# Conv matrices in pieces of 1 KB, five buffers for them in the second half of the convolution, and Silu pairs one group earlier

## The reference, cut to what matters

```python
def reference(x, ...):
    u = rms_norm(h, mix_pre_g)
    proj = u @ w_in                                    # 1024 -> 5120 columns
    a, gate = split(proj[..., :2048])
    c = a * sigmoid(gate)                              # GLU, 1024 channels
    c = depthwise_causal_conv(c, dw_kernel, dw_bias)   # 31 taps
    c = silu(layer_norm(c, conv_ln_g, conv_ln_b))
    y_conv = c @ w_conv_out
    y_pool = (pooled means of proj[..., 2048:3072]) @ pool_w * pool_scale @ w_pool_out
    g_conv, g_pool = sigmoid(proj[..., 3072:4096]), sigmoid(proj[..., 4096:])
    merged = g_conv * y_conv + g_pool * y_pool
    h = h + rms_norm(merged @ w_o, mix_post_g)
    v = square(relu(rms_norm(h, mlp_pre_g) @ w_ff1)) @ w_ff2
    return h + rms_norm(v, mlp_post_g)
```

## Time and profile before

| | us |
|---|---|
| median of 3 runs (lowest, highest) | 972.39 (970.23, 973.51) |
| the profiled execution's own time | 973.2 |
| its span, first to last instruction of the slowest core (core 7) | 971.6 |
| spans of cores 0 to 7 | 967.3, 962.5, 964.5, 968.4, 967.3, 964.5, 963.5, 971.6 |
| TensorE busy in that span | 947.4 (98%) |
| queue q0 (POOL): packets, MB | 55136, 46.45 |
| queue q1 (SP): packets, MB | 69792, 64.05 |

### The profile page before, as it was taken

The page is one execution under the profiler, slowest core; times in us unless marked ns, Lnnn a source line. Parts: engine busy times, 40 slices in busy tenths (PEclk is TensorE's granted clock), DMA queues, the critical chain, the costliest instruction groups (busy, mean ns, idle before and its releaser), DMA issues.

```text
span 971.6 us, 14273 instructions; the slowest of 8 cores (962.5 to 971.6 us)
## 1 busy us (share of the span) xinstructions
PE 947.4 (98%) x4990; PEld 479.7 (49%) x4990; DVE 405.3 (42%) x651; ACT 326.8 (34%) x592; POOL 42.4 (4%) x50
## 2 busy tenths in 40 slices
PE   5999999999989999999999999999999999999997
PEld 3555666775544444444444444444444444444444
DVE  3364232332647415675665541344323442333222
ACT  3565322111102492565544341133312341223211
POOL 3001000010110000010101000000000000000000
PEclk9999999999989999999999999999999999999999
DMA  9999602999999759569879994310242014210021
GB/s 193 217 218 177 77 1 46 138 155 144 126 121 177 131 123 148 112 143 234 152 195 177 201 177 109 98 65 1 66 127 93 19 26 116 96 47 1 1 87 66
DMA packets 125144, 111.69 MB, mean 115 GB/s; under 512 B 56945, under 2 KB 107377, under 8 KB 125074
## 3 DMA queue, kind: packets, MB, share of 16 engines
q0 software_dynamic: 55136, 46.45, 35.3%
q1 hardware_dynamic: 69792, 64.05, 25.7%
q10 hardware_dynamic: 146, 0.27, 0.1%
HBM read 127.78 MB, written 16.84 MB: 149 GB/s over the span
## 4 chain that ended last, share of the span: by engine, by line
PE 94%; DMA 4%; ACT 1%; issue 1%; DVE 0%; POOL 0%; DVEq 0%; ACTq 0%; POOLq 0%
PE ps L342 93%; DMA arena<-w_in 2%; DMA arena<-convw 2%; ACT arena L355 1%; PE ps L345 1%; ACT L355 0%; DVE arena L375 0%; POOL arena L378 0%; DVE arena L365 0%; DVEq L173 0%; ACT tmpA L355 0%; ACT junkb L355 0%; ACTq L140 0%; DVEq L140 0%; DVE sm L369 0%
## 5 line engine op out<-in xcount | busy, mean ns | idle before, releaser
L342 PE MATMUL ps<-arena 128*128 128x512 bf16 (+2 forms) x4560 | 916.8, 364 | 9.6 <-DMA arena<-convw 4.2
L342 PEld LDWEIGHTS ps<-arena 128*128 128x128 bf16 x4560 | 454.7, 104 | 464.3 <-issue 15.4
L355 ACT ACTIVATE tmpA<-ps 128x512 f32<-128x512 f32 x226 | 133.7, 595 | 343.2 <-PE ps L342 331.3
L358 DVE TENSOR_TENSOR arena<-tmpA 128x512 bf16<-128x512 f32 x128 | 88.2, 692 | 112.1 <-ACT tmpA L355 112.1
L358 DVE TENSOR_TENSOR arena<-ps,tmpA 128x512 bf16<-128x512 f32 x64 | 44.0, 691 | 151.8 <-ACT tmpA L355 133.5
L355 ACT ACTIVATE junkb<-ps 128x512 bf16<-128x512 f32 (+1 forms) x65 | 38.4, 591 | 177.5 <-DVE tmpA L358 112.7
L358 DVE TENSOR_TENSOR tmpA<-ps,gbt 128x512 f32<-128x512 f32 (+1 forms) x65 | 44.3, 681 | 34.3 <-PE ps L342 28.9
L355 ACT ACTIVATE junkb<-arena 128x1024 bf16<-128x1024 f32 (+1 forms) x33 | 34.6, 1050 | 60.6 <-DMA arena<-out 50.6
L358 DVE TENSOR_TENSOR sm<-sm 128x1 f32<-128x1 f32 x33 | 5.3, 160 | 108.5 <-ACT junkb L355 108.5
L355 ACT ACT_TABLE_LOAD x35 | 44.9, 1283 | 10.9 <-DVE mv L671 3.1
L355 ACT ACTIVATE arena<-ps 128x512 bf16<-128x512 f32 (+1 forms) x58 | 33.2, 586 | 36.2 <-PE ps L342 34.0
(11 more groups left out here) (40 smaller groups left out, 143.2 us busy)
## 6 DMA issues: line engine op xcount, KB each, us to landing
arena<-xh SPq DMA_DIRECT2D x32, 512.0 KB, 8.7
arena<-w_ff POOLq DMA_DIRECT2D x16, 1024.0 KB, 25.0
out<-arena SPq DMA_DIRECT2D x31, 512.0 KB, 3.0
arena<-out SPq DMA_DIRECT2D x28, 512.0 KB, 3.8
arena<-convw POOLq DMA_DIRECT2D x16, 768.0 KB, 13.0
arena<-w_in POOLq DMA_DIRECT2D x4, 1024.0 KB, 67.0
arena<-w_in POOLq DMA_DIRECT2D x2, 2048.0 KB, 22.6
arena<-w_in POOLq DMA_DIRECT2D x4, 512.0 KB, 20.3
```

Source lines behind the costliest of these rows:

```text
L342: kb.op("pe", lambda e: e.matmul(out_ap, lhsT=lhsT, rhs=rhs, start=start, stop=stop, skip_group_check=skip), reads=reads, writes=writes)
L355: kb.op("act", lambda e: e.activation(out=out_ap, in_=in_ap, func=func, **kw), reads=reads, writes=writes)
L358: kb.op(eng, lambda e: e.tensor_tensor(out=out_ap, in0=in0, in1=in1, op=op), reads=reads, writes=writes)
```

## The change

Three edits. The pieces of a conv load become twice as long (2 KB of f32, which land as 1 KB of bf16). Two more buffers for conv matrices are placed in the region of `S[1]`, which is free once the second GLU is done; loads 11 and 12 go there and are issued together ahead of the second half of the convolution, behind load 10 on POOL's queue. From load 8 on, load `w + 5` is issued behind `w`, and loads 13, 14 and 15 go to buffers 2, 0 and 1. Loads 0 to 10 keep their buffers and places. The load of `w_conv_out` waits for load 15 as before, which is now in buffer 1. The Silu pairs move to behind groups 22, 25, 28 and 30.

```diff
-        Wc = [aview(OFF_C + 4608 + b * 3072, 3072, g=8, d=3, n=128) for b in range(3)]
+        WC_OFF = [OFF_C + 4608, OFF_C + 7680, OFF_C + 10752, OFF_S + 8192, OFF_S + 11264]
+        Wc = [aview(o, 3072, g=8, d=3, n=128) for o in WC_OFF]
...
-        for b in range(3):
-            kb.reg(("Wc", b), (OFF_C + 4608 + b * 3072, 3072))
+        for b in range(5):
+            kb.reg(("Wc", b), (WC_OFF[b], 3072))
...
+        def wc_buf(w):
+            return {11: 3, 12: 4, 13: 2, 14: 0, 15: 1}.get(w, w % 3)
+
+        def cload(out_ap, in_ap, keys, after=()):
+            kb.op("pool", lambda e: e.dma_start(out=out_ap, in_=in_ap, max_dma_last_dim=2048), writes=keys, dma=True, after=after)
+
         def wc_load(w):
-            kb.op("pool", lambda e: e.dma_start(out=Wc[w % 3].rearrange("p g d n -> p (g d n)"), in_=convw[w // 2][:, (w % 2) * 3072:(w % 2 + 1) * 3072],
-                                                max_dma_last_dim=1024), writes=[("Wc", w % 3)], dma=True)
+            cload(Wc[wc_buf(w)].rearrange("p g d n -> p (g d n)"), convw[w // 2][:, (w % 2) * 3072:(w % 2 + 1) * 3072], [("Wc", wc_buf(w))])
...
-            if q % 2 == 1 and w + 3 < 16:
-                wc_load(w + 3)
+            nw = w + (3 if w < 8 else 5)
+            if q % 2 == 1 and nw < 16:
+                wc_load(nw)
...
         side1.pop(0)()
         side1.pop(0)()
+        wc_load(11)
+        wc_load(12)
         interleave(groups[:12], side1, 3)
-        wload(S[1][:, :, :], wco_v, ["wco"], after=[kb.last_write[("Wc", 0)]])
+        wload(S[1][:, :, :], wco_v, ["wco"], after=[kb.last_write[("Wc", 1)]])
...
-            if n in (23, 26, 29, 31):
-                i = (n - 22) // 3
+            if n in (22, 25, 28, 30):
+                i = (n - 21) // 3
                 silu_pair(i)
```

More of the change, by code:

```diff
@@ L652, in cv_mm @@
             w = cc * 2 + q // 2
+            wb = wc_buf(w)
             b = nb()
@@ L656, in cv_mm @@
                 for d in range(3):
-                    MM(ps[:, b, g4 * 128:(g4 + 1) * 128], UTt[bf][:, gl, 14 + d:142 + d], Wc[w % 3][:, gl % 8, d, :], d == 0, d == 2,
-                       [("UT", bf), ("UTh", bf), ("Wc", w % 3)], [PSK(b)])
+                    MM(ps[:, b, g4 * 128:(g4 + 1) * 128], UTt[bf][:, gl, 14 + d:142 + d], Wc[wb][:, gl % 8, d, :], d == 0, d == 2,
+                       [("UT", bf), ("UTh", bf), ("Wc", wb)], [PSK(b)])
             dst = ru[:, cc, :].rearrange("p (r g c) -> p g r c", r=16, g=16)[:, q * 4:q * 4 + 4, :, :]
```

## The result

The changed kernel takes 981.25 us (981.02 to 981.42, 4 runs); the kernel before takes 972.53 us beside it. The ratio is 1.0093, 95% interval [1.0075, 1.0111]: slower by 0.9%, where 969.1 us was forecast. The sets ran on different chips, so two experiments are compared by their ratios and not by their times.

What follows compares the result with a forecast made beforehand. TensorE's waits for loads, transposes and ScalarE on the four slowest cores were taken as the bound. After gains and a 2.2 us transpose price core 4 ends at 967.5, plus 1.6 between span and time: 969.1 us, range 964.5 to 976.0.

Steps and rivals of the forecast that it cites:

- The turn-taking: DMA engines alternate packet by packet between queues with work, so each transpose packet beside a load waits for one piece.
- part 2: Loads 11 and 12 beside the transposes of blocks 4 and 5: block 4's lands 2.2 us later on the slow cores.
- a share of 45%: Part of block 4's transpose taken to run beside a load, from core 0's packets: 0.45 x 4.9 = 2.2 us.
- the first rival: Block 4's transpose is paired with load pieces all along: price 4.9 us on cores 0 and 4, 975.1 us; chance 0.22.
- The slower rival: The packet pairs themselves are slow, 152 ns each, delaying block 4's transpose by 10.5 us: 980.7 us; chance 0.15.
- The step that failed: First half of the convolution: no load is added and half as many pieces are mixed in, so the cost is nothing.
- A second term: Block 5's transpose, used about 9 us after block 4's: loads and transposes are over by then, so no cost.
- the sum: Gains subtracted on cores 7, 3, 0 and 4, with 2.2 us added on cores 0 and 4; core 4 slowest at 967.5.
- The clock: Low clock behind core 7's block 7 stall: 3.4 us of TensorE's full-speed time lost, to be regained.
- Part 1's gain: Five buffers remove the convw stalls: 4.15 and 3.4 us of clock on core 7, 4.0 on core 3, about 1 elsewhere.
- parts 1 and 3: Five buffers end the convw waits; Silu pairs one group earlier end the 0.96 us ScalarE wait on all four cores.
- the fourth rival: Block 7's stall stays, for its transpose: 1.6 us and the lower clock on core 7, 969.7 us; chance 0.05.

Runs made afterwards that it cites:

- Experiment 6: The changed kernel with 1 KB landed pieces for loads 0 to 9 only, 512 bytes from load 10 on: 974.7 us, ratio 1.0023 to the kernel before.
- experiment 1: The changed kernel with pieces back at 512 bytes landed, five buffers and new Silu order kept: 968.86 us, ratio 0.9966 to the kernel before.
- experiment 5: The changed kernel with its pieces doubled once more, to 2 KB landed: 1005.95 us, ratio 1.0341 to the kernel before.
- experiment 2: The kernel before with only the pieces lengthened to 1 KB landed, three buffers and old Silu order kept: 982.7 us, ratio 1.0113.
- Experiment 7: The changed kernel with 512-byte landed pieces for loads 0 to 9, 1 KB from load 10 on: 975.6 us, ratio 1.0036 to the kernel before.
- Experiment 9: The changed kernel with 512-byte landed pieces and load 15 held until block 7's transpose lands: 967.3 us, ratio 0.9948 to the kernel before.

## Why the prediction was wrong

**Right.** The waits for `convw` and for ScalarE went, load 14 was issued at 249.34 us on core 7, and nothing waited for `w_conv_out`, whose load came 5.6 us earlier on core 7 and 4.8 later on core 4 (13 earlier was told). The turn-taking is as told, and its rate with 1 KB pieces, 148 a us, was measured as 147.

**Right by luck.** Block 4's transpose took 2.2 us longer on core 4 (15.4 to 17.6), the very figure of part 2. Over the eight cores it is 2.2 to 6.4, 3.4 on the mean, and core 3, where the price was to be nothing, now waits 3.86 us. The figure rests on a share of 45% read from one stretch of core 0; in the changed kernel the queues run nearly side by side through most of the transpose (1492 and 1649 packets from 238 to 250 us on core 4), as the first rival told. The slower rival had the sign and nearly the time (980.7), but its mechanism was a rate of 105 pairs a us, which isn't what happened.

**The step that failed** is the sentence "In the first half no load is added, and half as many pieces are mixed in: nothing." Its term was 0 and measured 5.5 us. The price of a longer piece was charged only where loads are added. But q1 takes turns with q0 wherever both have work, and block 2's transpose has loads beside it already before the change, with the halo's 16-byte packets ahead of it on its own queue. Experiment 6, which differs from experiment 1 in the pieces of loads 0 to 9 alone, gives the 5.5 us. That longer pieces cause it is shown; that the slower pace of the pairs is all of it is not, since on the slowest cores some 4 us of block 2's delay pass in the near standstill. The half of the sentence that sounds like a gain, fewer pieces to mix in, found no support: in experiment 5, with half as many pieces once more, the wait at block 2 grew to 15 us on three cores.

**A second term** was set to nothing: block 5's transpose "over by then". It stands behind block 4's on q1 and has loads 11 and 12 beside it, which the change itself put there; on core 4 it was 26.3 us on its way against 13.2 before. The placement alone lengthens it from 12.6 to 17.4 us on the mean of the cores, the long pieces then to 22.5 (table in experiment 2). It had more room than was told, too: block 5 comes about 13 us behind block 4 before the change (on core 7 the loads behind their first halves are issued at 244.30 and 257.34 us), not 9, because the reckoning left out the time of the `cv_mm` themselves. Experiment 7 gives 6.8 us for blocks 4 and 5 together, against 2.2 in the sum.

**The clock** was mis-sized in both directions. For the stall taken away on core 7 I took 3.4 us; but 10 us from its end have a clock of 0.72, so that only 2.8 were lost in work, the rest in idle time:

```profile
278.70:288.70 10.00, 10.00 (x70) 5.88 (x71) 3.38 (x6) 0.60 (x1) 1.12 (x2) 0.72 0.48 72
```

For the stalls put in the forecast took none, and each of core 4's three cost 1.7 to 2.7 us.

**Part 1's gain** was too large: 6.3 us for parts 1 and 3 together on the slowest core, 3.3 measured with small pieces. With small pieces the fourth rival, given 0.05, is what happened: load 14 comes in time and block 7's transpose holds TensorE for 2 to 4 us on five cores. Experiment 9 shows it in the traces, by holding load 15 back. (In the changed kernel itself the waits ahead of block 7 hide this one.) The 14.5 us on record for that transpose were seen, and explained away.

**The sum was made for four named cores of one run.** Core 7 was the slowest of that run and seldom of another (7 of 60), so the distance "to the next core" is no bound on what a change can gain or lose; what counts is how often any of the eight meets a late transfer.

What stays open: why some transposes crawl beside a load queue that moves next to nothing, as core 0's did between 233 and 238 us, and why both queues nearly stand still from 190 to 194 us on two cores in each of three kernels with long pieces (the changed one, experiments 2 and 6). No kernel was made for it.

## What to carry to other kernels

When a transfer's pieces are made longer, count the packets of everything that shares the DMA engines with it, over the whole stretch in which it runs and not only where the edit adds transfers: here each packet of the other queue waited for one piece on the mean, and the transposes (2048 packets of 256 bytes) and the halo (some 2000 of 16 bytes) paid for it. Where transposes and loads feed one pipeline, look for the slack of each in the trace (issue to landing, against issue to use) before helping one of them; here the loads had been late by 4 us on two cores and by 1 on two more, and block 4's transpose by 0.8 to 2.4 us on five. Holding back the single load that had time to spare took the last transpose off TensorE's path; holding all the late loads back only moved the wait. And where several cores run the same work, look at the slowest core of several runs before naming one that the change has to help.

## What the runs showed of the hardware that was not expected

The rate at which a transpose's packets pass beside a full load queue follows the landed piece closely: 333 a us at 256 bytes, 238 at 512, 147 at 1 KB, 82 at 2 KB. Over 16 engines that is 48, 67, 109 and 195 ns for each pair of packets: by a line through them, about 84 ns for each KB of the piece, on top of some 26 ns. The ratios of the four kernels go with it: 0.9951, 0.9966, 1.0093 and 1.0341. The two ends of that ladder are not alike: the times with 256 and 512 bytes can't be told apart, above 512 each doubling cost more than the one before. Beside 1 KB pieces packets of 16 bytes passed no faster (148 a us) than those of 256 bytes; beside 512-byte pieces they did (298 against 238).

A stall's price in clock is smaller than the low-clock stretch looks, since part of that stretch falls into the idle time itself: 2.1 us were lost in work behind the 4.88 us stall of core 4, and 1.7 behind the 2.03 us one. Not every stall has such a price: before the change core 4's 2.38 us were followed by 10 us at a clock of 0.83, core 3's 2.44 and 1.51 us by a clock of 1.00 (windows 267 to 277 and 273.3 to 283.3 us).
